# Values as the stationary operand, two heads in turn in the two column halves of the array, a ring of five logit rows, and weights loaded ahead of two seams

## The reference, cut to what matters

```python
mod = silu(c) @ w_ada + b_ada                 # six rows of 1024: shift, scale, gate, twice
h = rms_norm(x, g) * (1 + sc1) + sh1
qa, ka, va, cq, ckv, kidx, widx = split(h @ w_in)
# group A: window of two chunks of 64 keys, with a sink in the denominator
out_a = (softmax_with_sink(qa @ ka.T * s - slope * dist)) @ va
# group B: an indexer scores all visible keys, each query keeps 256 of them
score = sum_h w[q,h] * relu(qidx[q,h] @ kidx.T);  keep = top_k(score, 256)
out_b = softmax(masked(qb @ kb.T * s - slope * dist, keep)) @ vb
x = x + gt1 * rms_norm(concat(out_a, out_b) @ w_o)
h2 = rms_norm(x) * (1 + sc2) + sh2
x = x + gt2 * rms_norm((silu(h2 @ w_gate) * (h2 @ w_up)) @ w_down)
```

## Time and profile before

| what | value |
|---|---|
| time, median of 3 runs | 3321.71 us (3314.52 to 3324.0) |
| the profiled execution: its time, its span | 3318.27 us, 3316.5 us |
| PE, PEld busy | 2950.7 us (89%), 2411.2 us (73%) |
| DVE, ACT, POOL busy | 1688.8 us (51%), 1573.0 us (47%), 313.5 us (9%) |

### The profile page before, as it was taken

How to read it: one execution, slowest core, us unless ns; L and a number is a source line. 1 busy time by engine, 2 the same in 40 slices (tenths; PEclk the granted TensorE clock), 3 DMA queues, 4 the chain that set the end, 5 groups by cost and what they waited for, 6 DMA issues and landing times. The chain is left out here.

```text
span 3316.5 us, 42857 instructions
## 1 busy us (share of the span) xinstructions
PE 2950.7 (89%) x14649; PEld 2411.2 (73%) x14649; DVE 1688.8 (51%) x3080; ACT 1573.0 (47%) x3023; POOL 313.5 (9%) x990
## 2 busy tenths in 40 slices
PE   6678888787888888899896999999999999999997
PEld 2466666666676667788785887888878887888876
DVE  2246768686878867844454343244423443254422
ACT  0457787877787776875333222232223222232222
POOL 0012222212121210110011000000000000000000
PEclk8788888888998888789998999999999999999999
DMA  5000000000000000110555333343333432343323
GB/s 213 11 25 24 25 20 29 15 19 17 20 20 11 20 6 28 45 55 11 194 177 157 96 95 95 114 146 95 97 119 109 128 98 90 120 143 97 95 89 108
DMA packets 316074, 254.86 MB, mean 77 GB/s; under 512 B 9152, under 2 KB 271904, under 8 KB 315808
## 3 DMA queue, kind: packets, MB, share of 16 engines
q1 hardware_dynamic: 282544, 236.29, 22.9%
q10 hardware_dynamic: 33392, 16.81, 1.8%
HBM read 219.50 MB, written 33.57 MB: 76 GB/s over the span
## 5 line engine op out<-in xcount | busy, mean ns | idle before, releaser
L1962 ACT ACTIVATE p_hi<-raw 128x1024 fp32r<-128x1024 f32 x264 | 279.3, 1058 | 694.7 <-PE dbank L1933 355.7
L2036 DVE TENSOR_TENSOR p_lo<-raw,p_hi 128x1024 fp32r<-128x1024 f32 x264 | 323.4, 1225 | 426.6 <-ACT p_hi L1962 426.4
L1133 ACT ACTIVATE signs<-score,pick 128x512 int8<-128x512 f32 (+6 forms) x224 | 304.3, 1358 | 29.1 <-POOL pick L629 20.3
L1286 DVE TENSOR_SCALAR_CACHE_REDUCE above<-score,cand 128x384 uint8<-128x384 f32 (+6 forms) x224 | 315.8, 1410 | 4.3
L1111 ACT ACTIVATE logit<-tbank 128x512 f32<-128x512 f32 (+3 forms) x448 | 214.7, 487 | 207.5 <-PE tbank L847 203.8
L863 PE MATMUL obank<-vb,logit 128*128 128x64 f32 x2176 | 304.8, 286 | 0.0
L1914 PE MATMUL gbank<-x_hi,p_hi 128*128 128x512 f32 x704 | 275.5, 391 | 29.2 <-DVE p_lo L2036 29.2
L863 PEld LDWEIGHTS obank<-vb,logit 128*128 128x128 f32 x2176 | 298.8, 211 | 0.0
L1931 PE MATMUL dbank<-p_hi,a_hi 128*128 128x512 f32 x704 | 278.8, 396 | 17.0 <-DVE a_lo L2064 14.0
L847 PE MATMUL tbank<-ident,logit 128*128 128x128 f32 x1336 | 250.7, 301 | 42.9 <-ACT logit L1101 41.5
L729 PE MATMUL work<-w_in,h_T 128*128 128x512 f32 (+1 forms) x768 | 281.8, 514 | 0.7 <-ACT h_T L927 0.7
(11 more groups left out here) (219 smaller groups left out, 5240.2 us busy)
## 6 DMA issues: line engine op xcount, KB each, us to landing
raw<-in_w_gate_up SPq DMA_DIRECT2D x176, 512.0 KB, 3.8
raw<-in_w_down SPq DMA_DIRECT2D x88, 512.0 KB, 3.7
ada<-in_w_ada ACTq DMA_DIRECT2D x32, 512.0 KB, 3.8
wada<-in_w_ada SPq DMA_DIRECT2D x4, 2048.0 KB, 15.5
x_in<-in_x SPq DMA_DIRECT2D x16, 512.0 KB, 3.9
mixT<-oT SPq DMA_DIRECT2D x32, 256.0 KB, 2.3
mix<-mixT SPq DMA_DIRECT2D x16, 512.0 KB, 6.2
x_rows<-in_x SPq DMA_DIRECT2D x16, 512.0 KB, 4.6
```

Source lines behind the costliest of these rows:

```text
L1133: nc.scalar.activation(signs[:, 0:L], score[:, b % 2, 0:L], ACT.Sign, scale=-1.0, bias=pick[:].bitcast(F32), accum_out=less_more[:]).then_ ...
L1286: link(nc.vector.tensor_scalar(above[:, 0:L], score[:, b % 2, 0:L], cand[:].bitcast(F32), None, ALU.is_ge, ALU.add, accum_out=count[:]), b ...
L1962: nc.scalar.activation(p_hi[:, s], raw[:, s], ACT.Copy).then_inc(panel_high, 1)
L2036: nc.vector.tensor_tensor(p_lo[:, s], raw[:, s], p_hi[:, s].bitcast(F32), ALU.subtract).then_inc(panel_ready, 1)
```

## The change

- Values are now the stationary operand (128 keys x 64 channels) and the transposed probabilities move (128 columns). The result has 64 channels on its partitions: the even head of a pair goes to partitions 0 to 63 of `obank`, the odd one to 64 to 127, which is the left and the right half of the array's columns. The two heads' products are issued in turn, for each key tile. They stand a head later: all groups of four tiles but the last in the call of `head` with an even i (for heads i - 4 and i - 3), the last in the following one, ahead of that call's transposes.
- The output comes out turned already. Instead of four transposes of the scaled output, four transposes of the widened reciprocals (`turn_totals`) go through `tbank`; ScalarE copies them to `rtotal_T`, and VectorE multiplies `obank` with them straight into `oT`.
- The logit rows are a ring of five of 1920 elements; block 15's B heads use the memory of `w_in` and of a score row instead.
- `mod` has four steps instead of 32, each with 4 MB of `w_ada` in the memory of `w_in` and 32 products of 32 stationary and 256 moving columns. They stand beside B heads 1 and 5 of blocks 13 and 14. The bias and gain loads go to SP's queue.
- `w_o` and the first tile of `mixT` are loaded by SP during the last B block. The first tokens, the first two panels and the row of `ffn` are loaded ahead of the last two tiles of `project_output`.
- The split of the tokens in `ffn` is made in four parts instead of one copy and two subtractions, and the first product of a chunk waits for them one by one.

```diff
@@ weighted_values
-                pe.wait_ge(pt_ready, t + 1)
+                pe.wait_ge(pt_ready, plan.group0[i + 1] + g + 1)
...
                 for j, kt in enumerate(tiles):
-                    v = vb[:, kt, :] if kind == "B" else va[:, kt % 4, HD * (h // 4):HD * (h // 4 + 1)]
-                    mm = nc.tensor.matmul(obank[o % 2][:, h * HD:(h + 1) * HD], 
-                                          logit[:, i % 4, (4 * g + j) * P:(4 * g + j + 1) * P], v,
-                                          start=(g == 0 and j == 0), stop=(last and j == len(tiles) - 1))
+                    for r in range(2):
+                        v = vb[:, kt, :] if kind == "B" else va[:, kt % 4, HD * (h // 4):HD * (h // 4 + 1)]
+                        mm = nc.tensor.matmul(obank[o % 2][r * HD:(r + 1) * HD, h // 2 * P:(h // 2 + 1) * P], v,
+                                              row(i + r)[:, (4 * g + j) * P:(4 * g + j + 1) * P],
+                                              start=(g == 0 and j == 0), stop=(last and j == len(tiles) - 1))
@@ head(i) on TensorE
-                values = len(plan.groups(i - 3)) if 3 <= i < n + 3 else 0
-                for c in range(max(pieces, groups, values)):
+                pair = i - 5 if i % 2 else i - 4
+                values = len(plan.groups(pair)) if 0 <= pair < n else 0
+                first = max(values - 1, 1)
+                for c in range(max(pieces, groups, values, 1)):
                     if c < pieces:
                         piece(i, c)
+                    if c == 0 and i % 2:
+                        for g in range(first, values):
+                            weighted_values(pair, g)
+                    if c == 0 and 3 <= i < n + 3 and plan.heads[i - 3][2] == HEADS - 1:
+                        turn_totals(i - 3)
                     if c < groups:
                         transpose_group(i - 2, c)
-                    if c < values:
-                        weighted_values(i - 3, c)
+                    if i % 2 == 0 and c < min(first, values):
+                        weighted_values(pair, c)
@@ turn_totals, new
+                pe.wait_ge(rtotal_ready, OUT_ORDER.index((kind, b)) + 1)
...
+                for j in range(4):
+                    mm = nc.tensor.transpose(tbank[t % 2][:, j * P:(j + 1) * P], rtotal_wide[:, j, :], ident[:])
+                mm.then_inc(pt_full, 1)
@@ mod on TensorE
-                for k in range(KD):
-                    mm = nc.tensor.matmul(ps[:, 0:1], ada[:, k, :], shared.c_act[:, k:k + 1],
-                                          start=(k == 0), stop=(k == KD - 1))
+                for k in range(KD):
+                    for j in range(MOD_PARTS):
+                        mm = nc.tensor.matmul(ps[j * each:(j + 1) * each, 0:MOD_COLS],
+                                              shared.c_act[:, k:k + 1].to_broadcast([P, each]),
+                                              ada[:, k, j * MOD_COLS:(j + 1) * MOD_COLS],
+                                              start=(k == 0), stop=(k == KD - 1))
@@ logits on VectorE
-                if c == 0 and i >= 4:
-                    dve.wait_ge(pv_done, plan.group0[i - 3])
+                if c == 0 and i >= RING:
+                    dve.wait_ge(pv_done, plan.values_done(i - RING))
@@ output on VectorE: invert_totals for head i - 2, scale_output for head i - 4
+                dve.wait_ge(exp_done, i + 1)
...
+                nc.vector.tensor_copy(rtotal_wide.rearrange("p j (r d) -> p (j r) d", d=HD),
+                                      rtotal[:].unsqueeze(2).to_broadcast([P, HEADS, HD])
+                                      ).then_inc(rtotal_ready, 1)
...
+                nc.vector.tensor_tensor(oT[:], obank[o % 2][:].rearrange("p (j t) -> p j t", t=P), rtotal_T[:],
+                                        ALU.mult).then_inc(o_made, 1)
@@ SP, at the end of mixing and ahead of ffn
+                sp.wait_ge(pv_done, plan.values_done(plan.head_no["B", NB - 2, HEADS - 1]))
+                for k in range(KD):
+                    sp.dma_start(shared.later.w_o[:, k, :], w["w_o"][k * P:(k + 1) * P, :]).then_inc(shared.later.wo_in[k], 16)
...
+            sp.dma_start(ahead.x_lo[:].bitcast(F32), h2T_dram[:, :, 0:TOK]).then_inc(ahead.x_loaded, 16)
```

More of the change, by code:

```diff
@@ L405, in __init__, with values_done, turned_totals @@
                 v += SPLITS[s[0]]
+    def values_done(self, i):
+        pairs = self.heads[0:i // 2 * 2 + 1:2]
+        return sum(-(-len(key_tiles(kind, b)) // 4) for kind, b, _ in pairs)
+    def turned_totals(self, i):
+        return self.group0[i + 1] - 1
     def last_piece(self, kind, b):
@@ L544, in mixing, with row @@
         N_W = 8
+        def row(i):
+            k = i % RING
+            if plan.heads[i][0:2] != ("B", NB - 1):
+                return shared.later.rows[:, k * ROW:(k + 1) * ROW]
+            return w_in_flat[:, k * T:(k + 1) * T] if k < 4 else score[:, 0, :]
         def bias_of(kind, b, o, n):
@@ L919, in _ @@
                     i += 1
-            for j in range(5):
+            for j in range(4):
                 head(i + j)
@@ L1176, in _ @@
                     i += 1
-            for j in range(6):
+            for j in range(3):
                 head(i + j)
@@ L1456, with project_output @@
 OUT_ORDER = [("A", 0), ("A", 1)] + [o for b in range(NB) for o in (("A", b + 2), ("B", b)) if o[1] < NB]
-AFFINE_LOADS = 2 + sum(g is not None for g in MOD_GAINS)
+AFFINE_LOADS = MOD_PARTS * (1 + sum(g is not None for g in MOD_GAINS))
 N_CONST = 9
-def project_output(nc, w):
+def project_output(nc, w, later, ahead):
     with ExitStack() as ctx:
@@ L1498, in project_output @@
         rows_in = sem("rows_in")
-        wo_in = [sem("wo_in%d" % k) for k in range(KD)]
         wo_high = sem("wo_high")
@@ L1905, in _, with up_product @@
         def _(pe):
-            def up_product(c, j, s, which):
+            def up_product(c, j, s, which, begins=False):
                 n = 2 * j + which
@@ L1936, in chunk @@
             def chunk(c, first, last):
-                with pe.Fori(0, KF // 2) as jj:
-                    pe.wait_ge(x_split, 2 * (c + 1))
+                for s in range(2):
+                    for which in range(2):
+                        up_product(c, s, s, which, begins=(s == 0 and which == 0))
+                with pe.Fori(1, KF // 2) as jj:
                     for s in range(2):
@@ L2017, in chunk @@
                 if not last:
-                    x_high_part(c + 1)
+                    for part in range(4):
+                        x_high_part(c + 1, part)
                 for s in range(2):
@@ L2025, in _ @@
             nc.scalar.sem_inc(gated, 2)
-            x_high_part(0)
-            for s in range(2):
-                panel_high_part(0, 0, s)
+            for part in range(4):
+                x_high_part(0, part)
+                if part < 2:
+                    panel_high_part(0, 0, part)
             chunks(act, chunk)
@@ L2096, in chunk @@
                 if not last:
-                    x_low_part(c + 1)
+                    for part in range(4):
+                        x_low_part(c + 1, part)
                 for s in range(2):
@@ L2105, in _ @@
             nc.vector.sem_inc(act_ready, 2)
-            x_low_part(0)
-            for s in range(2):
-                low_part(s, s)
+            for part in range(4):
+                x_low_part(0, part)
+                if part < 2:
+                    low_part(part, part)
             dve.wait_ge(row_in, 16)
@@ L2137 @@
     w["x1"] = nc.dram_tensor("x1", (T, D), F32).ap()
-    with ExitStack() as ctx:
-        shared = Resident(ctx, nc)
-        modulation(nc, w, shared)
-        mixing(nc, w, shared)
-    project_output(nc, w)
-    ffn(nc, w)
+    with ExitStack() as kept_ctx:
+        kept = Kept(kept_ctx, nc)
+        with ExitStack() as later_ctx:
+            later = OutputWeights(later_ctx, nc, kept)
+            with ExitStack() as ctx:
+                shared = Resident(ctx, nc, kept, later)
+                modulation(nc, w, shared)
+                mixing(nc, w, shared)
+            project_output(nc, w, later, kept)
+        ffn(nc, w, kept)
     r = _run(nc, [arrays], core_ids=[0])
```

325 lines of the change are left out of this document (172 added, 153 removed).

## The result

The changed kernel takes 3334.6 us (median of 6 runs, 3332.8 to 3338.0), against 3316.7 for the one before on the same chip (6 runs): ratio 1.0052, 95% interval 1.0038 to 1.0065. It is slower by 0.5%, where I had forecast 3228 and a gain. The profiled execution took 3338.0 us, its span is 3336.2, 19.7 more than before.

The account below looks back on a forecast made before the run. Mixing was taken as bound by PE, VectorE and ScalarE in lockstep until 1240 us, by PE from 1377. Values 81, modulation 11, waits -20 and seams 20 took 92 off 3318.3: 3226, forecast as 3228 us, range 3178 to 3345.

Parts of the forecast that it names:

- Values, PE's time: Value products in mixing: the halves pair at 0.056 us a record, 183 us less PE work, 81 us gained.
- It doesn't hold the array for its length ... the trace shows no drain at that instance: Value products: one 32-column product, followed 0.03 us behind by a full one, justified the paired price without a drain.
- rival E: Rival: the array drains at each change between full and half, 86 us of PE, 43 at the end: 3271; chance 0.09.
- 1/3 from 200 to 1240 us: Mixing: worth of a saved PE microsecond there; the other shares are 1/4 to 1377 us and 0.8 after.
- Added waits, 20: Mixing: new waits between engines cost 20 us, all from the wait in `turn_totals`.
- (1): `turn_totals` waits once in eight heads for VectorE's reciprocals and copy: 0.6 us x 32 = 20.
- (3): Uneven calls, even ones up to 24 products, odd ones 8: cost nothing, up to 10 us if in turn.
- Modulation: Four steps in late mixing: 27 us of PE paired, load hidden; 13 gained before, 2 lost late, gain 11.
- Seams: Mixing to output projection gains 5.8 us, projection to feed-forward 14.2, by loading ahead; together 20.
- I leave as it is: TensorE's clock in mixing, 0.80 to 0.89 of full, taken as unchanged; could go either way by tens of microseconds.
- rival C: Rival: halves take turns; values gain nothing, modulation loses 10, uneven calls 10, waits 20, seams give 20: 3342; chance 0.16.

Follow-up runs that it names:

- g1: e2 with each head's value products alone in its own call, in one half, unpaired; ratio 1.0028 to the kernel before.
- k1: The kernel before, with the last tile's product of each value visit made as two of 64 stationary columns, one per half; 3435.8 us, ratio 1.0354.
- k2: The kernel before, with all value products made as two of 64 stationary columns, in turn into the two halves; 3311.7 us, ratio 0.9986.
- e4: The changed kernel, with a group's left-half products ordered ahead of its right-half ones; ratio 1.0099 to the kernel before.
- f2: e2 with all left-half products of a group ahead of its right-half ones; ratio 1.0002 to the kernel before.
- e2: The changed kernel, with the totals turned and copied a call later, at the call's end, and the multiplication one head later; ratio 0.9926 to the kernel before.
- f1: e2 with a pair's value groups shared evenly between its even and odd call; ratio 0.9889 to the kernel before.
- f3: e2 with only 4 of the 32 products of each modulation step; ratio 0.9890 to the kernel before.
- e3: The changed kernel, with PE turning a constant instead of the reciprocals, without waiting, outputs left unscaled; ratio 0.9897 to the kernel before.

## Why the prediction was wrong

**Values, PE's time: right in the main.** They pair at 0.109 us, PEld went from 374 to 168 us over the kernel, about the half forecast; PE's own busy time of these products is 227 us where near 190 was expected.

**"It doesn't hold the array for its length ... the trace shows no drain at that instance": this step failed.** I took one product of 32 columns as the nearest row and gave rival E 0.09. E had the price of a visit right: 2 x 0.16 us by its sum, 0.32 measured in g1. In the changed kernel itself, PE at full clock:

```profile
1604.06 0.51 PE L907 MATMUL lbank<-keys,qb_hi 128*128 128x512 f32 x1
...
1605.16 1.09 PE L951 MATMUL obank<-w_in,vb 128*64 128x128 f32 x16
1606.18 0.50 PE L907 MATMUL lbank<-keys,qb_hi 128*128 128x512 f32 x1
...
1610.10 0.48 PE L907 MATMUL lbank<-keys,qb_hi 128*128 128x512 f32 x1
1610.41 0.39 PE L908 MATMUL lbank<-keys,qb_lo 128*128 128x512 f32 x1
1610.65 0.60 PE L922 MATMUL tbank<-ident,w_in 128*128 128x128 f32 x4
1611.00 0.48 PE L907 MATMUL lbank<-keys,qb_hi 128*128 128x512 f32 x1
```

A step without values takes 0.90 us, one with a pair's four tiles 2.12: 1.22 for 16 records, where 16 x 0.056 = 0.90 was forecast and the kernel before spent 2 x 0.90. Of the 0.90 to be gained, 0.32 goes into the change. Over 224 visits that is 72 us of PE, at the shares of 0.3 to 0.45 some 22 to 32 of the end. "TensorEngine Tiling (Array Packing)" of the Trainium skill, section Key Properties, says that changing the tiling mode drains the array, and I had argued that away. The traces agree with it, by 0.32 us a visit in g1, 0.18 in k1 and 0.34 in k2.

**"1/3 from 200 to 1240 us" and the other shares: this step failed too.** I used 0.44 on the mean (81 of 183), and expected 92 us less of mixing from values and modulation. e4 and f2 show 0.3 and 0.45 for added time, which on the 156 us by which PE's value time fell would be 47 to 70. For saved time it is less: e2, without the wait, gains nothing up to 1190 us for 71 us of PE, where some 48 were forecast up to 1240, and mixing as a whole gives 3 us in e2 and 14 in f1. Three busy engines did not share the blame in thirds; when PE was done sooner it waited longer for VectorE. What sets the pace there in PE's place was not tested by a run that relieves VectorE or ScalarE.

**Added waits, 20: mis-sized.** (1) alone costs 42 to 51. I had priced 32 waits at 0.6 us, but between 200 and 1280 us 20 of them last 2.6 us each on PE, 51.2 together, and a wait is passed on through ScalarE and the search. (3), uneven calls "at nothing", is 12 us: in block 15 an even call lasts 7.2 us and an odd one 6.0.

**Modulation: better than forecast in PE's time** (21.0 us against 27), and its steps hide their loads (13.0 us to landing for 4 MB). But they stand late, where PE's time counts 0.7 by f3, while the products they replace stood in part where it counted nothing.

**Seams: right**, 18.6 us of 20.

**The clock, "I leave as it is": it moved.** From 200 us to the end of mixing the clock stood at 1.2 GHz for 451 us, 355 before, 376 in e2, 396 in e3, 352 in f1. The emptier PE, with its new waits, was granted less, and taking the waits away brought most of it back. The waits alone don't set it, for e4 keeps them and has 375. How many of e2's 42 us are the wait and how many the clock behind it, no run separates.

The distance from forecast to result is 109 us (92 forecast off, 17 on). The waits make 22 to 31 of it (42 to 51, less the 20 forecast), uneven calls 12. The other 66 to 75 us are the shares and the change of mode together, and f1, which has neither the wait nor the uneven calls, still lacks them. How they split stays open: at the shares of 0.3 to 0.45 the change of mode would be 22 to 32 of them, but where saved PE time was worth nothing, the change that ate some of it cost nothing either. That the result lies inside my range, and near 3342, the forecast of rival C, is chance: the halves do pair.

## What to carry to other kernels

Pairing two 64-column halves really halves the array time of such products, but each move from the full array to halves and back costs 0.18 to 0.34 us; count the visits, and set them against what one visit saves. Before an engine is made to wait for another, look at what that other engine does last before it signals: here a wait of 1.9 us on PE came back as 4.9 on ScalarE. Don't take the worth of an engine's time from busy shares. Measure it with a pair of runs, and in the direction that the change has: here added PE time cost 0.3 to 0.45 of itself, while 71 us saved ahead of 1190 us returned nothing.

## What was not expected of the hardware

- Two fp32 products with 64 stationary columns in the two column halves load and stream side by side: 0.109 us for a pair of records with 128 moving columns, 0.058 with 64 moving (k2), against 0.112 for one record with a load of 128.
- A change between full array and halves: 0.203 us from the last transpose to the first half product, where 0.109 stood. Back it is 0.203 with 128 moving columns (g1) and 0.152 with 64 (k2), where 0.084 stood. No load is made ahead.
- The granted clock doesn't follow PE's busy share: k1 had 157 us at 1.2 GHz with PE busy for 148 of them. g1, with unpaired products streaming longer, had a mean of 0.948, the changed kernel 0.911, the one before 0.921. It had 195 us at 1.2 GHz in mixing, against 355; how much of what being unpaired cost this repaid isn't measured.
